# Matrix memory laid between the tiles of the projection, its decay in fp32r, in a two-layer hybrid backbone

## The reference

```
b = cumsum(log_f);  dmat = b[:, None] - b[None, :] + log_i[None, :]   # lower triangle only
m_t = max(b + m_st, max(dmat));  w = exp(dmat - m_t) * (q @ k.T)
num = e_inter * (C @ q) + w @ v;  den = e_inter * (n . q) + sum(w)
h = num / max(|den|, exp(-m_t))          # chunk after chunk, forward and backward, summed
out = sigmoid(o_pre) * layernorm_per_head(h) * g
```

## Time and profile before

| | us |
|---|---|
| median of three runs (1578.15 to 1584.69) | 1584.53 |
| the profiled execution | 1577.79 |
| its span | 1576.0 |
| TensorE busy | 1430.5 (91%) |
| VectorE, ScalarE, GpSimd busy | 963.7, 595.0, 342.9 |
| granted TensorE clock, mean | 0.968 |

### The profile page before, as it was taken

How to read it: one execution, slowest core, us unless ns; L and a number is a source line. 1 busy time by engine, 2 the same in 40 slices (tenths; PEclk the granted TensorE clock), 3 DMA queues, 4 the chain that set the end, 5 groups by cost and what they waited for, 6 DMA issues and landing times.

```text
span 1576.0 us, 20293 instructions
## 1 busy us (share of the span) xinstructions
PE 1430.5 (91%) x7622; PEld 1142.7 (73%) x7622; DVE 963.7 (61%) x1353; ACT 595.0 (38%) x986; POOL 342.9 (22%) x272
## 2 busy tenths in 40 slices
PE   4699999798979999999988999576999999999996
PEld 2587877554448888888868998365788888878884
DVE  1844523576563434443458655653878978887985
ACT  2311123266030011010014115442767667676773
POOL 0108999930010000000001699600000000000000
PEclk9899999899989999999998999797999999999999
DMA  8236533274212322222231330005879779777840
GB/s 355 107 134 239 208 150 117 89 258 171 76 41 97 107 82 106 104 77 101 107 107 54 134 122 13 1 1 239 345 300 366 277 292 376 274 284 323 336 183 27
DMA packets 30305, 267.06 MB, mean 169 GB/s; under 512 B 3360, under 2 KB 3360, under 8 KB 4256
## 3 DMA queue, kind: packets, MB, share of 16 engines
q1 hardware_dynamic: 30240, 266.15, 44.3%
HBM read 265.09 MB, written 1.05 MB: 169 GB/s over the span
## 4 chain that ended last, share of the span: by engine, by line
PE 73%; DVE 8%; POOL 8%; ACT 6%; issue 4%; DMA 1%; DVEq 0%; ACTq 0%; SPq 0%
PE ps L460 35%; PE ps L820 13%; PE ps L840 6%; POOL sb_arena L1783 4%; PE ps L706 4%; POOL sb_arena L1786 3%; PE ps L473 2%; PE ps L790 2%; DVE sb_rows_n L1482 1%; PE ps L490 1%; PE ps L799 1%; PE ps L592 1%; DMA sb_arena<-mod 1%; PE ps L579 1%; PE ps L639 1%
## 5 line engine op out<-in xcount | busy, mean ns | idle before, releaser
L460 PE MATMUL ps<-sb_h_hi,sb_w_hi 128*128 128x512 f32 (+1 forms) x640 | 241.8, 378 | 9.8 <-DVE sb_h_lo L1300 9.8
L460 PE MATMUL ps<-sb_h_lo,sb_w_hi 128*128 128x512 f32 (+1 forms) x640 | 240.8, 376 | 0.0
L460 PE MATMUL ps<-sb_h_hi,sb_w_lo 128*128 128x512 f32 (+1 forms) x640 | 240.7, 376 | 0.0
L1299 DVE CAST sb_w_hi<-sb_arena 128x2048 fp32r<-128x2048 f32 (+1 forms) x58 | 74.2, 1279 | 212.5 <-PE ps L460 139.6
L1783 POOL TENSOR_SCALAR sb_arena<-sb_arena,sb_small 128x512 f32<-128x512 f32 (+1 forms) x120 | 176.2, 1468 | 11.8
L460 PEld LDWEIGHTS ps<-sb_h_hi,sb_w_hi 128*128 128x128 f32 x640 | 121.8, 190 | 32.1 <-DVE sb_h_lo L1300 10.6
L820 PE MATMUL ps<-sb_egu_lo,sb_h_lo 128*128 128x512 f32 (+1 forms) x384 | 143.4, 374 | 0.0
L1786 POOL TENSOR_TENSOR sb_arena<-sb_arena 128x512 f32<-128x512 f32 (+1 forms) x120 | 138.6, 1155 | 10.0
L460 PEld LDWEIGHTS ps<-sb_h_hi,sb_w_lo 128*128 128x128 f32 x640 | 121.7, 190 | 21.9
L460 PEld LDWEIGHTS ps<-sb_h_lo,sb_w_hi 128*128 128x128 f32 x640 | 121.8, 190 | 21.5
L1300 DVE TENSOR_TENSOR sb_w_lo<-sb_arena,sb_w_hi 128x2048 fp32r<-128x2048 f32 (+1 forms) x58 | 134.2, 2314 | 2.0
(11 more groups left out here) (288 smaller groups left out, 2815.4 us busy)
## 6 DMA issues: line engine op xcount, KB each, us to landing
sb_arena<-experts SPq DMA_DIRECT2D x90, 1536.0 KB, 8.7
sb_arena<-mod SPq DMA_DIRECT2D x48, 1024.0 KB, 5.6
sb_arena<-in SPq DMA_DIRECT2D x24, 1024.0 KB, 4.9
sb_arena<-gate SPq DMA_DIRECT2D x11, 1024.0 KB, 4.8
sb_arena<-up SPq DMA_DIRECT2D x11, 1024.0 KB, 4.7
sb_arena<-out SPq DMA_DIRECT2D x8, 1024.0 KB, 4.8
sb_arena<-down SPq DMA_DIRECT2D x8, 1024.0 KB, 4.8
sb_arena<-down SPq DMA_DIRECT2D x4, 768.0 KB, 4.2
```

Of the source, the lines that this page charges most:

```text
L460: ins = pe.matmul(o, left[a], right[b], start=(k == first and n == 0), stop=(k == final and n == len(PRODUCTS) - 1))
L1299: settled(v.tensor_copy(hi, x), ("hi", key))
```

## The change

The memory's work is cut into 16 steps, four a head (keys; decay forward; decay backward; sums forward, the backward sums going with the next head's keys), and one step is laid behind every half chunk of the projection from the fifth chunk on, on all three engines. cg and ca go ahead of mv. The moments are taken head by head. The decay's operands are fp32r: `pick` and masks are rounded once; the rows are kept as leading bits (partitions 0 to 63) and remainder (64 to 127), and `pick` has its ones in both halves, so that one product adds both. From the fourth chunk on ScalarE makes w_hi (`lead`) and VectorE only the remainder (`split_rest`). The fillers that stood in the memory go to the attention: three ahead of its first turn, and two instead of one in steps 0 to 4. CONV_STEP becomes 10 and 6. A Sqrt on a spare element stands ahead of five waits. The diff's core, with unchanged bodies left out:

```diff
-CONV_STEP = (7, 3)
+CONV_STEP = (10, 6)
-IN_ORDER = ["mk", "mq", "mv", "cg", "ca", "ak0", "ak1", "aq0", "aq1", "av0", "av1", "mo"]
+IN_ORDER = ["mk", "mq", "cg", "ca", "mv", "ak0", "ak1", "aq0", "aq1", "av0", "av1", "mo"]
+MEMORY_FROM = 4
+LEAD_FROM = 3
-LATE_MOD = {n: (8 + 2 * j, 9 + 2 * j) for j, n in enumerate(IN_ORDER[3:11])}
+LATE_MOD = {n: (8 + 2 * j, 9 + 2 * j) for j, n in enumerate(IN_ORDER[2:10])}
...
+        def attention_steps(l):
+            return max(NH * (NB - low(l) // P) + 2, CONV_STEP[l] + 5)
...
@@ TensorE, project(l)
+                            if b % 2 and step >= 0:
+                                memory_step(l, step + b // 2)
...
+                            if step >= 0:
+                                memory_step(l, step + m)
...
+                memory_sums(l, NH - 1, 1)
...
+            def memory_decay(l, h, d):
+                if (h, d) == (0, 0):
+                    pe.wait_ge(*act_done.at(("rows_r", l)))
+                    pe.wait_ge(*dve_done.at(("rows_lo", l)))
...
+                            pe.matmul(o[:, s * P:(s + 1) * P], pick_r[:, row, :],
+                                      rows_r[:, j, s * P:(s + 1) * P], start=True, stop=False)
+                            ins = pe.matmul(o[:, s * P:(s + 1) * P], ident_r[:, :], mask_r[d], start=False, stop=True)
+                        for x, y in spans:
+                            ins = pe.matmul(o[:, x * P:y * P], pick_r[:, row, :],
+                                            rows_r[:, j, x * P:y * P], start=True, stop=True)
...
+            def memory_step(l, step):
+                h, part = divmod(step, 4)
+                if step == 0:
+                    memory_columns(l)
+                if part == 0:
+                    if h:
+                        memory_sums(l, h - 1, 1)
+                    memory_keys(l, h)
+                elif part < 3:
+                    memory_decay(l, h, part - 1)
+                else:
+                    memory_sums(l, h, 0)
...
@@ TensorE, attention(l)
                 scores(0)
-                for n in range(len(units) + 2):
+                fill(l, 3)
+                memory_turn(l)
+                for n in range(attention_steps(l)):
...
-                    fill(l, 1)
+                    fill(l, 1 + (n < 5))
...
@@ ScalarE, project(l)
                 for n, name in enumerate(IN_ORDER):
-                    if name == "mv":
+                    if n + 1 in range(LEAD_FROM, len(IN_ORDER)):
+                        lead(("in", l, IN_ORDER[n + 1]))
+                    if n == 2:
                         act.wait_ge(*dve_done.at(("row_m", l)))
...
+            def lead(chunk):
+                n, c = slot_of[chunk], split_of[chunk]
+                act.wait_ge(*pe_done.at(last_product(split_chunks[c - SPLIT])))
+                act.wait_ge(sem_slot[n % RING], 16 * (n // RING + 1))
+                f(w_hi[:, c % SPLIT], chunk_view(chunk), ACT.Copy).then_inc(*act_done.tick(("lead", chunk)))
...
+                            act.wait_ge(*dve_done.at(("rows_lo", l)))
+                            f(rows_r[0:64], rows_n[0:64, 0:NB, :], ACT.Copy).then_inc(*act_done.tick(("rows_r", l)))
...
+            def memory_deviation(l):
+                f(spare, eps, ACT.Sqrt)
+                act.wait_ge(*dve_done.at(("hvar", l, NH - 1)))
...
@@ VectorE, gate_rows(l)
+                v.tensor_copy(ident_r[:, :], ident)
...
-                split(("in", l, IN_ORDER[3]))
+                split_rest(("in", l, IN_ORDER[3]))
...
+                split_rest(("in", l, IN_ORDER[4]))
+                conv_input(l)
                 dve.wait_ge(*act_done.at(("row_em", l)))
...
+                settled(v.tensor_copy(kq_r[0:64], rows_n[0:64, 0:NB, :]), ("rows_hi", l))
+                v.tensor_tensor(rows_r[64:128], rows_n[0:64, 0:NB, :], kq_r[0:64].bitcast(F32), ALU.subtract)\
+                    .then_inc(*dve_done.tick(("rows_lo", l)))
...
@@ VectorE, project(l)
+                    if n < MEMORY_FROM:
+                        continue
+                    step = 2 * (n - MEMORY_FROM)
+                    if n + 1 < len(IN_ORDER):
+                        split_rest(("in", l, IN_ORDER[n + 1]))
+                    if step:
+                        memory_step(l, step - 1)
+                    if IN_ORDER[n - 1] in ("ak0", "ak1", "aq0", "aq1"):
                         rope(l, IN_ORDER[n - 1])
+                    memory_step(l, step)
+                memory_step(l, step + 1)
...
+            def memory_output(l):
+                memory_sums(l, NH - 1, 1)
+                memory_moments(l, NH - 1)
                 dve.wait_ge(*act_done.at(("hstd", l)))
...
+            for name in ("pick", "mask_f", "mask_b"):
+                ins = v.tensor_copy(rounded(name), field(con, CONST, name))
+        pick[64 + 32 * (r // NH) + r % NH, r] = 1.0
```

More of the change, by code:

```diff
@@ L163, in build @@
             u_hi_mid = sb("u_hi_mid", [P, 2, T], F32R, over)
+        with ExitStack() as over:
+            kq_r = sb("kq_r", [P, NB, T], F32R, over)
         kq = sb("kq", [P, NB, T])
@@ L167, in build @@
             wg_hi = sb("wg_hi", [P, KD, GATE_ROWS], F32R, over)
+        with ExitStack() as over:
+            rows_r = sb("rows_r", [P, NB, T], F32R, over)
         with ExitStack() as over:
@@ L596, in mlstm, with memory_keys @@
[L596 to L604 removed]
+                pe.wait_ge(*act_drained.at(("mq", l, 1)))
+            def memory_keys(l, h):
+                r0, m = DH * (h % 2), h // 2
+                for s in range(NB):
+                    a = max(low(l), CTX if s >= 2 else 0)
+                    o = open_bank(("kq", l, h, s))
+                    pe.matmul(o[:, a:T], mk[r0:r0 + DH, m, s * P:(s + 1) * P], mq[r0:r0 + DH, m, a:T],
+                              start=True, stop=True).then_inc(*pe_done.tick(("kq", l, h, s)))
@@ new lines, in project @@
+                            if step >= 0:
+                                memory_step(l, step + m)
+                    if l == 0:
+                        for i in LATE_MOD.get(name, ()):
+                            modulation_rows(0, i)
+            def lead(chunk):
[3 more added lines that the diff above has]
+                f(w_hi[:, c % SPLIT], chunk_view(chunk), ACT.Copy).then_inc(*act_done.tick(("lead", chunk)))
@@ new lines, in memory_decay @@
+            def memory_decay(l, h, d):
+                col = 32 * d + h
+                if h:
+                    act.wait_ge(*pe_done.at(("pv", l, h - 1, d)))
+                elif d == 0:
+                    act.wait_ge(*dve_drained.at(("cols", l)))
+                for s in range(NB):
+                    o = full(("dec", l, h, d, s))
+                    for a, b in block_pairs(d, s, l):
+                        ins = f(W[:, d, s, a * P:b * P], o[:, a * P:b * P], ACT.Exp,
+                                bias=cols[:, 0, s, col:col + 1])
+                    ins.then_inc(*act_drained.tick(("dec", l, h, d, s)))
@@ new lines, in memory_step @@
+            def memory_step(l, step):
+                h, part = divmod(step, 4)
+                if part == 0:
+                    memory_keys(l, h)
+                elif part < 3:
+                    memory_decay(l, h, part - 1)
+            def memory_deviation(l):
+                f(spare, eps, ACT.Sqrt)
+                act.wait_ge(*dve_done.at(("hvar", l, NH - 1)))
+                g = low(l) // P * NH
+                f(stat[:, 2, g:], stat[:, 1, g:], ACT.Sqrt, scale=1.0 / DH, bias=eps).then_inc(*act_done.tick(("hstd", l)))
@@ new lines, in memory_step @@
+            def memory_step(l, step):
+                h, part = divmod(step, 4)
+                if step == 0:
+                    memory_columns(l)
+                if part == 0 and h:
+                    memory_sums(l, h - 1, 1)
+                    memory_moments(l, h - 1)
+                elif part in (1, 2):
+                    memory_weights(l, h, part - 1)
+                elif part == 3:
+                    memory_sums(l, h, 0)
+            def memory_output(l):
+                t0 = low(l) // P
+                memory_sums(l, NH - 1, 1)
+                memory_moments(l, NH - 1)
+                dve.wait_ge(*act_done.at(("hstd", l)))
+                settled(v.reciprocal(stat[:, 3, t0 * NH:NB * NH], stat[:, 2, t0 * NH:NB * NH]), ("hrstd", l))
+                for m in range(2):
+                    x = hsum[m][:, t0:NB]
+                    r = stat[:, 3, :].rearrange("p (b h) -> p b h", b=NB)[:, t0:NB, 2 * m:2 * m + 2]
+                    v.tensor_tensor(x, x, r.unsqueeze(3).to_broadcast([P, NB - t0, 2, DH]), ALU.mult)\
+                        .then_inc(*dve_done.tick(("hn", l, m)))
```

250 lines of the change are left out of this document (114 added, 136 removed).

## The result

The changed kernel takes 1566.59 us (median of 8 runs, 1557.06 to 1577.58); the kernel before takes 1579.12 beside it (8 runs). The ratio is 0.992, 95% interval 0.9896 to 0.9944: faster by 12.5 us, or 0.8%, which is clear of the noise; 38 us were forecast, and the time lies just above the range (1565). The profiled execution took 1566.26 us, span 1564.5; TensorE's mean granted clock fell from 0.968 to 0.958.

What follows compares the result with a forecast made beforehand. It took TensorE's own instructions to bound layer 0's memory and GpSimd's convolution to set layer 1's mixer end. Gains of 19 us in each layer, 38 in all, gave a forecast of 1543 us, range 1524 to 1565.

Steps and rivals of the forecast that it cites:

- Decay in fp32r: Layer 0's memory: narrow fp32r products at 0.21 us each, a head 4.9 us less, 19.6 us (to 26.4) for four heads.
- What interleaving adds: Layer 0's projection with memory steps between: waits for weights, a late-drained bank and order slips add 6 us.
- the granted clock as before: Sign of being right: TensorE's granted clock stays unchanged; no size given.
- The hole (−7): End of layer 0's memory: TensorE's 10.1 us hole shrinks to 3 us with moments by head, 7 us less.
- they cancel: Eight modulation chunks leave layer 0's memory and come back in its attention, so no net time.
- DMA in the attention (+1.5): Layer 0's attention: two modulation chunks per step ask for transfers faster than they come, 1.5 us more.
- Layer 1 (19): Layer 1: earlier convolution and fewer attention steps after it bring the output 20 us earlier, 19 taken.
- Small edits: Rounding of pick and masks, early Sqrt and sigmoid table loads: nothing; without cover the loads 2.6 us a layer.
- the slower one: Rival, chance 0.03: TensorE waits for weights at each sum in both layers, 66 us against 44 gained, 1603 us.
- All of it: Rival, chance 0.03: VectorE's 53 us of work stops GpSimd in layer 1, convolution 166 us, total 1572 us.
- the waits at the sums: Sign of being right: in layer 0 TensorE's sums wait for weights about 1 us.
- the wait at conv_mean: Sign of being right: in layer 1 TensorE waits under 2 us for the convolution at conv_mean.

Runs made afterwards that it cites:

- e4: The changed kernel with the decay's products computed as f32 again, all else left; 1568.97 us.
- e1: The changed kernel with ScalarE's copy and VectorE's remainder moved later, behind memory work of the step; 1549.13 us.
- e10: The changed kernel with seven unread f32 products in each of TensorE's two holes at the end of layer 0's memory; 1554.48 us.
- e2: The changed kernel with another order at the memory's end: two modulation chunks drained before the moments' wait, four ahead of the turn; 1556.25 us.
- e5: The changed kernel with VectorE making both parts of every chunk and ScalarE copying nothing; 1569.80 us.
- e11: The changed kernel with the memory's steps behind the projection again in both layers; 1568.77 us.
- e9: The changed kernel with layer 1's convolution input taken later, after the memory's rows and mv's first tile; 1566.06 us.

## Why the prediction was wrong, step by step

**Decay in fp32r (19.6 us): right in kind, size too small.** TensorE's work fell by 26 us, the far end of what I gave (26.4); the narrow products lie below its 0.12 us, at 0.06 to 0.11. Some 11.5 of the 26 come with the 128 partitions, which I did not price; fp32r alone gives 15, less than my term. But I counted work on TensorE as time, and in the changed order it was not: e4 puts fp32r's own 15 us at 2.4 there.

**"What interleaving adds": +6. This is the step that failed.** My picture was right and its sizes nearly so. In the chunk above the product starts at 178.0; from there lead is ready at 9.2 us (I had 8.3), the weights at 14.7 (13.6), and TensorE wants the sums at 12.5 (12.9), because the decay is shorter than I costed. That makes 2.2 us of wait where I had 0.7 and booked 1; I had no wait for the keys' bank (4.4 us, gone in e1), and nothing for what a wait does to the clock. From 84 to 285 us the waits come to 11.5 us against my 6, and some 24 us at half the clock make, as an estimate, up to 12 more. The load is tied to the chunk's end, so shorter work on TensorE became more of both. Three chunks take 73.6 us where 59.3 would do (e1), and output 0 comes 20.3 us later than in e1's order, which does the same work.

**The clock: not in the sum at all.** I wrote "the granted clock as before". In the changed kernel's layer 0 each wait of 1.6 us or more came with 1.2 GHz, and at the end of the memory this alone took some 10 us (e10). The kernel before showed it: its clock falls to 0.50 inside the 10.1 us hole and is still 0.50 from 308 to 314 us, with TensorE at work. I split a hole in two and booked 7 us; but the old hole had 6 us of slow work behind it, and the two new ones have over 20 between and behind them.

**The hole (−7) and the modulation chunks ("they cancel").** The holes did shrink from 10.1 to 6.5 us. The chunks did not cancel: they were moved from a stretch at full clock into the one at half, 0.86 us more each. The cause I named for the first hole, ScalarE standing at the last moment ahead of its evictions, was the right one, and e2 removes that hole.

**DMA in the attention (+1.5).** No wait of TensorE for a load shows there. The 2.9 us at L510 is a wait for ScalarE.

**Layer 1 (19): 17.2 measured.** The convolution ends 5.4 us nearer to layer 0's output, and 11.8 come from the shorter way from there to the output (forecast 11.5). The first tap came 9.4 us nearer to layer 0's output, forecast 10. The convolution took 137.1 us instead of the 133 I kept, and TensorE waited 4.7 us for it, where I had under 2. That it sets layer 1's end is borne out by e5 (longer by 6, wait 12.0), and e11 shows that TensorE would be next without the interleaving.

**Small edits.** None was tried alone. The table loads at 268 to 276 us, for the sigmoid beside Exp, cost TensorE no wait.

**The rivals.** The one that named the right place was the slower one: TensorE waits for the weights at each sum. It was priced at 66 us, with a rope and 3.3 us or more at every sum, and got 0.03; the true case lay between it and my +6. "All of it" did not come: it had a convolution of 166 us, and it took 137.1, with the casts back 143.0. Changed kernel, VectorE and GpSimd in layer 1:

```profile
903.28 2.39 DVE L1390 TENSOR_TENSOR sb_w_lo<-sb_arena,sb_w_hi 128x2048 fp32r<-128x2048 f32 x1 [4.24 <-ACT sb_w_hi L1061]
...
903.62 2.84 POOL L1900 TENSOR_SCALAR sb_arena<-sb_arena,sb_small 128x256 f32<-128x256 f32 x1
```

GpSimd's product takes 0.93 us when free; here it starts during VectorE's remainder and ends 0.8 us after it. The Trainium skill, SBUF — State Buffer, "Who interferes with whom", has the loser of the port blocked fully; for the long remainders this trace agrees, with some 2 us lost at each. What was wrong is the rival's sum, which charged the short weights and ropes at full length too: in all the convolution lost 24 us (137.1 less 113), not 53.

With both orders mended the total comes near my sum: output 0 at 378.3, 22.6 earlier than before (forecast 19), and 1538.6 us in all (forecast 1543). That is partly luck, for the decay's work fell by 7 us more than its term and holes with slow clock are left. None of the three signs that I had named for being wrong came (sums waiting 3 us each, a convolution over 145 us, a decay over 7 us a head). Of the signs for being right the clock, the waits at the sums and the wait at conv_mean failed. I had watched the length of single waits and not their price.

## What to carry to other kernels

When a change puts work that waits for a DMA into a queue, ask what stands behind it there, and whether the load's issue waits for that in turn: such a loop swallows whatever an engine saves. Price an idle gap of TensorE with what follows it, not by its length alone: here useless products in two gaps of 3 us made the kernel 12 us faster, though not every gap of this length slowed the clock. And before counting a faster instruction as time, ask in which order of the queues its engine is the one that is waited for.

## What the runs showed that I had not expected

- Gaps of 2 to 3 us were enough for a granted clock of 0.50 (1.2 GHz). At the end of the memory it lasted some 7 us (e2), 27 us (the change) or 61 us (e9's run), with gaps of 2.1 to 3.3 us. Two gaps of 2.15 and 2.45 us of the kernel before left it at 1.00.
- fp32r products of 128 columns cost 0.06 to 0.11 us from start to start, f32 ones 0.22 with all operands on 128 partitions, and 0.31 to 0.42 where products with operands on 64 and on 128 alternate.
- The convolution on GpSimd took 132.9 us (e9), 137.1 (the change) and 143.0 (e5) for the same instructions; a remainder of VectorE (2.3 us) held up the GpSimd instruction it met by some 2 us.
